# Attention value products on the two column halves of TensorE, in two groups a head instead of four

## The reference

```
def block(args):
    qn, qr = args
    sc = (jnp.einsum("bqhd,bkhd->bhqk", qn, k_nope)
          + jnp.einsum("bqhr,bkr->bhqk", qr, k_rope))
    p = jax.nn.softmax(sc.astype(jnp.float32) * scale, axis=-1).astype(v.dtype)
    return jnp.einsum("bhqk,bkhd->bqhd", p, v)
```

## Time and profile before

| what | value |
|---|---|
| median of 3 runs | 2745.19 us |
| the profiled execution's own time | 2745.84 us |
| its span | 2744.1 us |
| TensorE (PE) busy | 2699.8 us (98%) |
| TensorE weight loads (PEld) busy | 2201.2 us (80%) |
| VectorE (DVE) busy | 1441.6 us (53%) |
| GpSimd (POOL) busy | 1835.0 us (67%) |
| ScalarE (ACT) busy | 834.9 us (30%) |
| the attention's heads, layer 1 and 2 | about 120 to 210 us and 715 to 805 us |

### The profile page before, as it was taken

How to read it: one execution, slowest core, us unless ns; L and a number is a source line. 1 busy time by engine, 2 the same in 40 slices (tenths; PEclk the granted TensorE clock), 3 DMA queues, 4 the chain that set the end, 5 groups by cost and what they waited for, 6 DMA issues and landing times.

```text
span 2744.1 us, 40422 instructions
## 1 busy us (share of the span) xinstructions
PE 2699.8 (98%) x14166; PEld 2201.2 (80%) x14166; DVE 1441.6 (53%) x1967; ACT 834.9 (30%) x1393; POOL 1835.0 (67%) x1812
## 2 busy tenths in 40 slices
PE   8999999999999999999999999999999999999999
PEld 6778888888788888887777778888877777888887
DVE  7886544327867444245766563021558875611225
ACT  3554222101653222014656231010143331300202
POOL 6576777776657777766555559687575555777864
PEclk9999999999999999999999999999999999999999
DMA  4212332332113232322222223233232222232322
GB/s 156 70 32 70 100 99 95 105 104 91 46 40 100 95 97 98 102 86 96 70 74 70 93 69 115 93 99 97 80 108 69 70 70 66 81 106 94 99 93 70
DMA packets 66790, 237.63 MB, mean 87 GB/s; under 512 B 7424, under 2 KB 7936, under 8 KB 66624
## 3 DMA queue, kind: packets, MB, share of 16 engines
q1 hardware_dynamic: 65792, 234.00, 26.3%
q10 hardware_dynamic: 832, 1.51, 0.2%
HBM read 233.38 MB, written 2.10 MB: 86 GB/s over the span
## 4 chain that ended last, share of the span: by engine, by line
PE 87%; DVE 6%; issue 2%; DVEq 2%; ACT 2%; DMA 0%; ACTq 0%; POOL 0%; POOLq 0%; SPq 0%
PE ps L482 27%; PE ps L488 26%; PE ps L485 26%; DVE ps L1939 1%; PE ps L656 1%; PE ps L1255 1%; PE ps L1213 1%; DVE negmax L2050 1%; PE ps L1073 1%; PE ps L895 1%; PE ps L1065 1%; PE ps L1068 0%; DVEq L1826 0%; DVEq L2668 0%; PE ps L988 0%
## 5 line engine op out<-in xcount | busy, mean ns | idle before, releaser
L435 POOL TENSOR_SCALAR w_hi<-w_raw 128x512 fp32r<-128x512 f32 x437 | 283.6, 649 | 836.0 <-PE ps L482 739.6
L482 PE MATMUL ps<-x_hi,w_hi 128*128 128x512 f32 (+1 forms) x1872 | 744.0, 397 | 8.0 <-DVE x_lo L2403 2.3
L488 PE MATMUL ps<-x_hi,w_lo 128*128 128x512 f32 (+1 forms) x1872 | 731.1, 391 | 0.0
L485 PE MATMUL ps<-x_lo,w_hi 128*128 128x512 f32 (+1 forms) x1872 | 730.8, 390 | 0.0
L440 POOL TENSOR_TENSOR w_lo<-w_raw,w_hi 128x512 fp32r<-128x512 f32 x437 | 614.7, 1407 | 0.0
L438 POOL TENSOR_TENSOR w_lo<-w_raw,w_hi 128x512 fp32r<-128x512 f32 x437 | 599.4, 1372 | 0.0
L482 PEld LDWEIGHTS ps<-x_hi,w_hi 128*128 128x128 f32 x1872 | 353.3, 189 | 89.0 <-issue 10.6
L485 PEld LDWEIGHTS ps<-x_lo,w_hi 128*128 128x128 f32 x1872 | 353.2, 189 | 74.7 <-issue 4.3
L488 PEld LDWEIGHTS ps<-x_hi,w_lo 128*128 128x128 f32 x1872 | 353.2, 189 | 73.8
L436 POOL TENSOR_SCALAR w_hi<-w_raw 128x512 fp32r<-128x512 f32 x437 | 305.9, 700 | 0.0
L482 PE MATMUL ps<-a_hi,w_hi 128*128 128x512 f32 x512 | 200.3, 391 | 0.0
(11 more groups left out here) (442 smaller groups left out, 4521.4 us busy)
## 6 DMA issues: line engine op xcount, KB each, us to landing
w_raw<-wts SPq DMA_DIRECT2D x437, 512.0 KB, 3.4
xres<-xT SPq DMA_DIRECT2D x2, 1024.0 KB, 8.1
outT<-xres SPq DMA_DIRECT2D x7, 256.0 KB, 2.0
pf<-pT ACTq DMA_DIRECT2D x2, 512.0 KB, 4.8
prm<-prm SPq DMA_DIRECT2D x1, 438.5 KB, 9.5
lev<-levels ACTq DMA_DIRECT2D x1, 384.0 KB, 4.6
outT<-xres SPq DMA_DIRECT2D x2, 128.0 KB, 1.7
wtmp<-pos SPq DMA_DIRECT2D x1, 128.0 KB, 2.6
```

Of the source, the lines that this page charges most:

```text
L435: nc.gpsimd.tensor_scalar(w_hi[:, s, a], w_raw[:, s, a], 1.0, 0.0, ALU.mult, ALU.add).then_inc(w_rounded[s], 1)
L482: mm = nc.tensor.matmul(out, whi, xhi, start=first, stop=False)
L485: mm = nc.tensor.matmul(out, whi, xlo, start=False, stop=False)
L488: return nc.tensor.matmul(out, wlo, xhi, start=False, stop=last)
```

## The change

Each product of 128 queries becomes two of 64 queries: the one goes to the first 64 columns of the array and writes the PSUM partitions 0 to 63, the other goes to the last 64 and writes the partitions 64 to 127. Both go through the same four tiles of keys, taking turns. The elements that are computed and the bank in which they land are the same. And `weighted` isn't called behind each `scores` any more, but twice in a row behind the second and twice behind the fourth. The four of the last head stay together.

```
                     for kt in range(TT):
-                        mm = nc.tensor.matmul(ps[5][:, qt * VW:(qt + 1) * VW], p_t[:, h % 2, kt, qt * P:(qt + 1) * P],
-                                              v_sb[:, kt, h, :], start=kt == 0, stop=kt == TT - 1)
+                        for r in (0, P // 2):
+                            c = qt * P + r
+                            mm = nc.tensor.matmul(ps[5][r:r + P // 2, qt * VW:(qt + 1) * VW], p_t[:, h % 2, kt, c:c + P // 2],
+                                                  v_sb[:, kt, h, :], start=kt == 0, stop=kt == TT - 1)
                     if qt == TT - 1:
                         mm.then_inc(pv_done, 1)
...
-                        if h:
+                        if h and kt % 2:
+                            weighted(h - 1, kt - 1)
                             weighted(h - 1, kt)
...
                 for kt in range(TT):
-                    if kt == 0:
-                        weighted(last - 1, 0)
                     scores(last, kt)
-                    if kt:
+                    if kt % 2:
+                        weighted(last - 1, kt - 1)
                         weighted(last - 1, kt)
```

## The result

The changed kernel takes 2749.89 us (median of 20 runs, 2745.08 to 2753.69), the kernel before 2745.39 us (20 runs beside it, 2742.2 to 2748.71). The ratio is 1.0014, with a 95% interval of 1.0008 to 1.0021: slower by 3.8 us (the medians lie 4.5 us apart, the means 3.8 us). Forecast were 2744.2 us, 1 us faster than before, and a range of 2741 to 2749.5 us. So the sign was wrong, and the time lies 0.4 us outside the range.

What follows compares the result with a forecast made beforehand. VectorE was taken to pace the third to sixth heads, TensorE the attention's end. 2745.84 us (profiled execution) − 2.2 (two tails) + 1.2 (one clock fall) = 2744.8, less 0.65 to the median: 2744.2 us; range 2741 to 2749.5 us.

Steps and rivals of the forecast that it cites:

- VectorE paces heads two to six, gain 0: Loops with `h` 1 to 5: VectorE's list is full, so TensorE's saving of 0.3 us a head becomes waiting; gain 0.
- A double group 1.3 us, the last head's four 2.2 us: `weighted` on TensorE: two groups fall from 1.80 to 1.3 us, the last head's four from 3.6 to 2.2 us.
- The first `coarse` waits 0.7 us: Each head's first `coarse`, now directly behind the first `scores`: TensorE stands 0.7 us for ScalarE's `q_hi`.
- Waits before L628 of 0.8, 1.2, 1.6, 1.1, 2.2 us: TensorE's waits before `max_row` for `h` 1 to 5, where the saved time and the old waits gather.
- The tail, −1.1 us a layer: From the seventh head on TensorE decides: `row_stat` at 209.1 instead of 210.24 us, 1.1 us gained a layer.
- Six such waits in two layers; I count one fall, +1.2 us.: Longer waits before L628 (1.6, 2.2 us) and `row_stat` (1.2 us) may lower TensorE's clock; one fall counted, +1.2 us.
- the clock falls more often: Rival, waits before L628 and `row_stat`: 1.2 to 1.6 us a fall; three give 2747.5 us, six 2752; 23%.
- Range: 2741 to 2749.5 us, taking in the forecast and three to four falls; 2 in 10 left outside.

Runs made afterwards that it cites:

- the filled kernel: Changed kernel plus unused products of a constant in heads one to five and in the last head's four `weighted`; 2743.68 us, ratio 0.9988 to the kernel before.
- the order alone: Kernel before with two `weighted` in a row behind the second and fourth `scores`, products still of 128 queries; 2750.18 us, ratio 1.0013.
- `query` first in the kernel before: Kernel before with only `query(h + 2)` put before `max_row(h + 1)` from the second head on, no halves or filling; 2748.44 us, ratio 1.0011.

## Why the prediction was wrong

- *VectorE paces heads two to six, gain 0.* Right: the two traces are 1.97 us apart before and 1.95 us behind these heads.
- *A double group 1.3 us, the last head's four 2.2 us.* Right: 1.28 us, and from 206.86 + 0.23 to 209.54 − 0.23 (the starts of the products around it) 2.22 us. The rule of the Trainium skill ("TensorE: Matmul & The Clock Gate", Part 3), that a weight load runs beside a matmul in flight only when their row groups differ, doesn't hold for this pair of halves: all products here use all 128 rows, and a pair costs 0.058 us where one 128-column load with its matmul took 0.112.
- *The first `coarse` waits 0.7 us.* Right, 0.6 us by the trace (0.4 in the second head).
- *Waits before L628 of 0.8, 1.2, 1.6, 1.1, 2.2 us.* Right in order, somewhat high: 0.60, 0.93, 1.48, 0.94 and 1.84 us.
- *The tail, −1.1 us a layer.* Right: −1.06 and −1.08 us (0.25 + 0.83), with `scores` waiting 1.25 us for `mrow` and `row_stat` 0.96 us for VectorE (forecast: 1.2 us each).
- *The clock: "Six such waits in two layers; I count one fall, +1.2 us."* This is the step that failed, and with it the sign. The places were right, and a fall costs 1.55 to 1.6 us, the upper end of the 1.2 to 1.6 that I gave it (the sum had taken the lower). Their number was wrong: 5.8 us of clock were lost in the mean, some 3.4 falls; the profiled execution had three, two of them behind the two `row_stat` and one behind the four longest waits before L628. The rival "the clock falls more often" is what happened, 2747.5 us for three falls and 2749 for four; it had 23%. I had put the new waits between an idle stretch that kept the clock (1.2 us) and one that lost it (2.3 us), and so counted on their length. The length doesn't sort them: waits before L628 of up to 1.84 us kept the clock 11 times in 12, a wait of 1.83 us in the trace of before (at 1999.72 us) kept it too, and waits of 1.0 to 1.4 us before `row_stat` lost it 6 times in 8. What stands out is what follows: behind `row_stat`'s wait come eight matmuls of one column. In the trace of before the same kind had lost the clock after a wait of 1.12 us (products 0.42 us apart from 1968.84 us on), and once with hardly any wait, ahead of the slow products of the earlier trace rows:

```profile
1966.08 1.05 PE L836 MATMUL ps<-ones,ssum 128*128 128x1 f32 x8 [1.12 <-DVE ssum L2491]
...
1968.84 0.63 PE L482 MATMUL ps<-p_hi,w_hi 128*128 128x512 f32 x1
1969.26 0.63 PE L485 MATMUL ps<-p_lo,w_hi 128*128 128x512 f32 x1
```

```profile
1604.64 1.05 PE L836 MATMUL ps<-ones,ssum 128*128 128x1 f32 x8 [0.24 <-DVE ssum L2491]
1605.56 1.03 PE L840 MATMUL ps<-ones,root 128*128 128x1 f32 x8
```

Whether these one-column matmuls are what matters isn't shown: no run took them away and kept the wait.

- *Range.* Its upper end took in three to four falls, and the median came to 2749.89, 0.4 us beyond it.

What stays open: how often the waits before L628 lose the clock, and whether the half groups themselves help to lose it. Groups of halves with full work around them kept it (the double groups at full clock in the filled kernel), but no run held the waits constant and changed only the width of the products.

## What to carry to other kernels

Work taken from an engine that doesn't set the pace turns into idle time, and on TensorE idle time isn't free: where waits of 1 to 2 us gather, count the stretches at the lower clock, and price each at its products times the 0.2 us that it adds (1.6 us here), before the saving is counted. Here the waits to look at first were those with one-column matmuls behind them, before `row_stat`. Products that nobody uses, put into the waits, delayed nothing here (the fourth head's `max_row` and `row_stat` stood where they had) and turned 3.8 us lost into 3.3 us gained; those before `row_stat` alone brought the clock back. And before an order is changed, list what each moved piece covers (`q_hi`, `mrow`, the square sums): it was the cover, not the work, that cost with the order alone and with `query` first in the kernel before.

## What the runs showed of the hardware

- In the trace of the changed kernel, pairs of 64-column fp32 products with 65 moving columns on the two column halves start together (0.01 us apart), and the pairs follow each other every 0.06 us in the group of 64 matmuls: 2.09 us less the last one's 0.22 us are 31 distances; the same work in 128-column products took 0.112 us for each load and matmul. With four accumulating key tiles it is no slower than in L1232.
- A group of halves between products of 512 columns costs more than its pairs: 0.82, 1.28 and 2.22 us for 8, 16 and 32 pairs, some 0.35 us beyond 0.058 us a pair. So fewer and larger groups are cheaper.
- The busy share doesn't tell the clock: TensorE is 98% busy in both kernels, and the tenths of the clock on the profile's page read alike (all 9), while the mean granted clock went from about 0.9955 to 0.9934 and took 5.8 us.
- The same program differs by 6 us between runs (2742.2 to 2748.7 us in 20), and one part of it may be where the stretches fall in the first 40 us: the traces before and after were 1.97 us apart before any instruction that differed.
